# An opening stage in place of three, four modulation rows moved into projection 1, the experts' down products in split form, and their weights loaded as 8 KB by partition

## What is computed

```python
sh1, sc1, gt1, sh2, sc2, gt2 = split(silu(c) @ w_mod + b_mod, 6)       # w_mod 1024 x 6144; c_ctx likewise
h  = rms_norm(x, g_pre_mix) * (1 + sc1) + sh1                          # ctx likewise, with its own two
u, uc = h @ w_in, hc @ w_in                                            # w_in 1024 x 4544
# first experts: 16, each on its 128 best tokens
hid = silu(xs @ w_gate) * (xs @ w_up); ye = hid @ w_down * gate        # three of 1024 x 1024
# second experts: 32 of width 512, slots of 128 tokens
gate, up = split(xs @ w_gate_up); ye = (silu(gate) * up) @ w_down      # 1024 x 1024 and 512 x 1024
```

## Time and profile before

| | |
|---|---|
| three runs | 5071.03, 5068.59, 5067.89 us, median 5068.59 |
| the profiled execution | 5070.47 us, its span 5068.4 us |
| mean granted TensorE clock | 0.909 |
| busy | PE 4206.1 us (83%), DVE 2385.4 (47%), ACT 1724.3 (34%), POOL 406.9 (8%) |
| DMA | 845.85 MB, mean 167 GB/s |

### The profile page before, as it was taken

One profiled execution on the slowest core, in us unless ns is written; L12 is line 12 of the kernel. 1 busy time (PEld: TensorE's weight loads), 2 busy tenths in 40 slices (PEclk: granted clock), 3 DMA queues, 4 the chain that ended last, 5 costly groups with the idle time before them and its releaser, 6 DMA issues. The chain is left out here.

```text
span 5068.4 us, 73757 instructions
## 1 busy us (share of the span) xinstructions
PE 4206.1 (83%) x30161; PEld 2975.7 (59%) x30161; DVE 2385.4 (47%) x3865; ACT 1724.3 (34%) x3214; POOL 406.9 (8%) x376
## 2 busy tenths in 40 slices
PE   4999966869886738999949999777779886499995
PEld 1788844448885616667538444566634655266673
DVE  2211154566664665656441464316610345466664
ACT  2211022645543304444231343216610233244442
POOL 0000012210002100000000231000000000100001
PEclk7999976979998869999969999889989998799997
DMA  6222131652223419999742332231121223699997
GB/s 246 88 93 89 62 119 48 173 162 81 78 78 117 142 68 366 367 367 367 248 183 83 119 107 78 87 113 38 38 83 50 100 58 125 237 382 381 385 382 286
DMA packets 414050, 845.85 MB, mean 167 GB/s; under 512 B 35136, under 2 KB 235872, under 8 KB 410392
## 3 DMA queue, kind: packets, MB, share of 16 engines
q1 hardware_dynamic: 393240, 782.68, 43.0%
q0 software_dynamic: 12032, 41.96, 2.6%
q10 hardware_dynamic: 8448, 16.56, 1.0%
HBM read 676.74 MB, written 164.36 MB: 166 GB/s over the span
## 5 line engine op out<-in xcount | busy, mean ns | idle before, releaser
L390 PE MATMUL psum<-proj_hi,proj_w 128*128 128x512 f32 (+2 forms) x1728 | 460.7, 355 | 15.2 <-DVE proj_w L430 13.0
L2452 ACT ACTIVATE moe_hi<-moe_raw 128x2048 fp32r<-128x2048 f32 x128 | 245.0, 1917 | 301.9 <-PE psum L2403 248.7
L2660 PE MATMUL psum<-qkv_w,hT 128*128 128x512 f32 x768 | 336.2, 597 | 12.4 <-DMA qkv_w<-in_w_in 12.4
L390 PEld LDWEIGHTS psum<-proj_hi,proj_w 128*128 128x128 f32 (+1 forms) x1728 | 303.8, 188 | 65.2 <-DVE proj_w L430 13.4
L2487 DVE TENSOR_TENSOR moe_lo<-moe_raw,moe_hi 128x2048 fp32r<-128x2048 f32 x128 | 291.5, 2288 | 87.1 <-ACT moe_hi L2452 85.1
L390 PE MATMUL psum<-proj_lo,proj_w 128*128 128x512 f32 (+2 forms) x864 | 306.1, 354 | 0.0
L4028 DVE TENSOR_TENSOR moe_lo<-moe_raw,moe_hi 128x2048 fp32r<-128x2048 f32 x128 | 287.0, 2285 | 33.4 <-ACT moe_hi L3994 33.4
L2660 PEld LDWEIGHTS psum<-qkv_w,hT 128*128 128x128 f32 x768 | 145.7, 192 | 190.3 <-issue 177.5
L3994 ACT ACTIVATE moe_hi<-moe_raw 128x2048 fp32r<-128x2048 f32 x128 | 237.1, 1905 | 11.6 <-DMA moe_raw<-in_w_gate_up 11.2
L3248 PE MATMUL psum<-branches_T,mixed_w 128*128 128x512 f32 x512 | 221.9, 596 | 13.7 <-DMA mixed_w<-in_w_attn_o 13.7
L2413 PE MATMUL psum<-moe_wd,moe_hidT 128*128 128x512 f32 x512 | 224.3, 596 | 8.4 <-DVE moe_hidT L2508 8.4
(11 more groups left out here) (612 smaller groups left out, 8697.0 us busy)
## 6 DMA issues: line engine op xcount, KB each, us to landing
moe_raw<-in_w_gate_up SPq DMA_DIRECT2D x128, 1024.0 KB, 16.4
moe_raw<-in_w_gate SPq DMA_DIRECT2D x64, 1024.0 KB, 6.9
moe_raw<-in_w_up SPq DMA_DIRECT2D x64, 1024.0 KB, 7.4
moe_wd<-in_w_down SPq DMA_DIRECT2D x64, 1024.0 KB, 9.4
moe_wd<-in_w_down SPq DMA_DIRECT2D x32, 2048.0 KB, 11.0
mod_w<-in_w_mod SPq DMA_DIRECT2D x24, 1024.0 KB, 13.9
uT<-proj_out SPq DMA_DIRECT2D x35, 640.0 KB, 2.9
chunks_pr<-prim SPq DMA_DIRECT2D x40, 512.0 KB, 4.1
```

Of the source, the lines that this page charges most:

```text
L390: ins = nc.tensor.matmul(bank[e * nch + c][0:width, 0:n], l, r, start=(k == 0 and i == 0), stop=(k == KD - 1 and i == 2))
L2452: nc.scalar.activation(hi[:, n % R], raw[:, n % R], ACT.Copy).then_inc(s["hi_ready"], 1)
L2660: last = nc.tensor.matmul(bank[2 * (n % 2) + c_][:, :], hT[:, k, i * P:(i + 1) * P], w[:, m % 2, k, c_ * BANK:(c_ + 1) * BANK], start=(k = ...
```

## The change

*Opening.* `modulation` and two `norm_T` become one stage, `opening`. It loads the first 8 pieces of `w_mod` alone (shift and gain of the first norm, for c and c_ctx), then the 10 tiles of ctx and x. The rows stay on chip: small transposes turn them into columns (`gs`). ScalarE's and VectorE's work on the tiles is the same as before.

*Later rows.* The other four rows (`Later`) are made in `gemm_T`, from 32 pieces of 128 x 1024 that are loaded into the free `hT`, ring of 4. VectorE, after each group's copy and split, does three pieces (`w * c + total`, a column of silu(c) by partition); after 8 pieces TensorE sums over partitions with a column of ones, two products of one column by 512 into banks 6 and 7, before groups 4, 7, 9 and 12, and VectorE finishes the row, SP stores it.

*Experts.* Both use one ring for all weights (`raw`, 8 and 10 pieces of 1 MB), and `w_down` pieces pass `top` and `rest` like the others. `hid` transposed is split too (`hT_hi` by ScalarE, `hT_lo` by VectorE). Down is then 48 split products in the first experts, 24 in the second. A piece's rows are laid out by `(p k) n`: partition p holds rows 2p and 2p+1, one stretch of 8 KB, and the transposes of tokens and `hid` take every other column to match. In the second experts the store of an expert's `ye` now stands in SP's order behind the loads of the third expert after it.

```diff
-def modulation(nc, bank, w_mod, b_mod, cvec, gains, mod, tables):
+def opening(nc, bank, cst, w_mod, b_mod, cvec, gains, tables, sc, ctx, x, hT):
...
-                for i in range(SETS * KD):
+                for i in range(KD):
                     if i >= R:
                         sp.wait_ge(used, i - R + 1)
+                    sp.dma_start(w[:, i % R, :], w_mod[0, i * P:(i + 1) * P, 0:PIECE]).then_inc(w_in[i % R], 16)
+                for i in range(N):
+                    src = ctx[i * P:(i + 1) * P, :] if i < NTC else x[(i - NTC) * P:(i - NTC + 1) * P, :]
+                    sp.dma_start(xt[:, i, :], src).then_inc(x_in[i], 16)
...
+                dve.wait_ge(b_in, 16 * 2 * COLT)
+                dve.wait_ge(gain_in, 16 * COLT)
+                dve.wait_ge(used, KD)
+                for j in range(COLT):
+                    nc.vector.tensor_tensor(m[at(j), :], bank[0][at(j), :], bias[at(j), :], ALU.add).then_inc(shift, 1)
...
+                for j in range(COLT):
+                    dve.wait_ge(cols_mm, j + 1)
+                    nc.vector.tensor_copy(gs[:, j // 2, 4 * (j % 2):4 * (j % 2) + 4, :].rearrange("p k r -> p (k r)"),
+                                          bank[(1, 2, 3, 0)[j]][:, 0:8]).then_inc(cols, 1)
...
+class Later:
+    ROWS = ((MOD_GT1, 1), (MOD_S2, None), (MOD_G2, 2), (MOD_GT2, 3))
+    PER, RING = 3, 4
...
+    def turn(self, v):
+
+        return (KD * v + KD - 1) // self.PER + 2
...
+                    if later is not None:
+                        for p in range(later.PER * g, later.PER * (g + 1)):
+                            load_piece(p + later.RING)
...
+                def sums(v):
+                    pe.wait_ge(piece_done, KD * (v + 1))
+                    for j in range(2):
+                        last = nc.tensor.matmul(bank[6 + j][32 * v:32 * v + 1, :], later.one,
+                                                actT[:, 4 + v % 2, j * BANK:(j + 1) * BANK], start=True, stop=True)
+                    last.then_inc(sum_mm, 1)
...
+                        ins = nc.vector.scalar_tensor_tensor(total, w_p, c, total, ALU.mult, ALU.add)
...
-    GU, R = 8, 4
+    RAW, R = 8, 4
...
-            return m[e, 2 * j * P:2 * (j + 1) * P, :].rearrange("(k p) n -> p k n", p=P)
+            return m[e, 2 * j * P:2 * (j + 1) * P, :].rearrange("(p k) n -> p k n", k=2)
...
+        def columns(k):
+
+            return ds(k // 2 * 2 * P + k % 2, P, step=2)
...
-                        down(e - 1)
+                        for j in range(4):
+                            of_down(e - 1, j)
...
-    GU, R, RD = 4, 6, 2
+    RAW, R = 10, 4
```

More of the change, by code:

```diff
@@ L161, in _ @@
[L161 to L172, removed]
@@ L360, in load, with load_piece @@
                         .then_inc(w_in[g % 2], 16)
+                def load_piece(p):
+                    if p >= later.PIECES:
+                        return
+                    if p >= later.RING:
+                        sp.wait_ge(piece_done, p - later.RING + 1)
+                    v, k = p // KD, p % KD
+                    c = later.column(v)
+                    sp.dma_start(actT[:, p % later.RING, 0:D], later.w_mod[0, k * P:(k + 1) * P, c:c + D])\
+                        .then_inc(piece_in[p % later.RING], 16)
                 load(0)
                 load(1)
+                if later is not None:
+                    sp.wait_ge(x_lo, KD)
+                    for v, (dst_row, gain) in enumerate(later.ROWS):
+                        c = later.column(v)
+                        sp.dma_start(row(6, v), later.b_mod[0:1, c:c + D]).then_inc(row_in, 16)
+                        if gain is not None:
+                            sp.dma_start(row(7, v), later.gains[0:1, gain, :]).then_inc(row_in, 16)
+                    sp.wait_ge(row_in, 16 * 7)
+                    for p in range(later.RING):
+                        load_piece(p)
                 for g in range(G):
@@ L376, in _ @@
             def _(pe):
+                def sums(v):
[4 more added lines that the diff above has]
+                    last.then_inc(sum_mm, 1)
                 for g in range(G):
+                    for v in range(0 if later is None else len(later.ROWS)):
+                        if g == later.turn(v):
+                            sums(v)
                     pe.wait_ge(lo_ready, g + 1)
@@ L442, in _ @@
                         rest(g + 2)
+                    if later is not None:
+                        for p in range(later.PER * g, later.PER * (g + 1)):
+                            piece(p)
+                        for v in range(len(later.ROWS)):
+                            if g == later.turn(v):
+                                finish(v)
 class Loop:
@@ L3887, in experts2_own, with turn, gate_up, down @@
         gate_bank, up_bank, h_bank, x_bank, y_bank = bank[0], bank[1], bank[2], bank[3:5], bank[5:7]
+        def turn(e):
+            return 6 * e - 2 if e else 0
+        def gate_up(e, j):
+            return turn(e) + j
+        def down(e, j):
+            return turn(e + 1) + (4 if e + 1 < E2 else 0) + j
+        def rows(m, e, j):
+            return m[e, 2 * j * P:2 * (j + 1) * P, :].rearrange("(p k) n -> p k n", k=2)
+        def columns(k):
+            return ds(k // 2 * 2 * P + k % 2, P, step=2)
         with nc.Block() as block:
```

556 lines of the change are left out of this document (325 added, 231 removed).

## The result

| | before | changed |
|---|---|---|
| median of 4 runs | 5069.81 us (5067.89 to 5072.50) | 4947.19 us (4941.17 to 4949.40) |
| ratio | | 0.9754, 95% interval 0.9742 to 0.9767 |
| the profiled execution | 5070.47 us | 4941.17 us, its span 4939.2 |

The forecast was 4955, its range 4915 to 5008. The time lies inside; the two expert terms do not lie where the forecast had them.

A forecast was written before the change was run, and what follows sets the result against it. In both experts stages TensorE and DMA were taken to end together; the opening filled neither. 63 - 7 + 32 + 25 = 113 us off the profiled 5070.5 gave 4957.5, adjusted to the median as 4955 us, range 4915 to 5008.

The forecast's parts named there:

- Opening, -63 forecast: Opening: projection 1 would begin at 63.9 instead of 126.8 us, saving 63 us, between 58 and 65.
- Later rows, +7 forecast: Projection 1: TensorE's sums for the four later rows add 7 us, at most 9; the rest is hidden.
- VectorE's 41 us: Projection 1: 32 VectorE operations of 1.28 us for the later rows, hidden while it waits 396 us for TensorE.
- Split down: Both experts: split down products and quicker transfers gain 32 us in the first, 25 us in the second.
- Of the period 4.2 us are lost to mixed traffic ... so I keep some 3 us: 35.3: First experts: transfers set the new period at 35.3 us, a gain of 2.0 an expert, 32 us in all.
- All three lie within 1.7 us; I take 18.4: Second experts: TensorE, VectorE and transfers nearly tie, period 18.4 us, gain 0.77 an expert, 25 us in all.
- the DMA share is 1.00 and 1.01: two resources end together: Both experts before the change: TensorE always busy and DMA full too, at about 367 and 382 GB/s.
- TensorE remains the bound: Rival for both experts, 20%: mixed stretches quicken too, gains of 45 and 45 us, time 4923 us.
- the second rival: Both experts: periods of 34.5 and 17.8 us would prove it, TensorE remaining the bound; 20%.
- the bad case: Both experts: the two-column step doubles the transposes, adding 1.6 and 1.1 us an expert, floors 36.1 and 18.9.
- The ceiling of 358 GB/s: Rival for both experts, 5%: the HBM path limits loads whatever their stretch, periods stay, time 5013 us.
- that rival's half clock: Rival for both experts, 3%: brief TensorE waits drop its clock to half, one piece each costing 131 us.

The follow-up runs named there:

- the run with dearer pieces: The changed kernel with each of the 32 later-row pieces in projection 1 passed over twice more by VectorE; 4943.57 us.
- the thinned 4 KB kernel: The changed kernel with 4 KB stretches, contiguous transposes, one split product of three in the experts and no VectorE rests of weights; 4888.34 us.
- the thinned 8 KB kernel: The changed kernel with one split product of three in the experts and no VectorE rests of weights, 8 KB stretches kept; 4887.97 us.
- small rings: The changed kernel with raw weight rings of 4 and 6 pieces instead of 8 and 10; 5042.72 us beside 5083.80 of before.
- the 4 KB run: The changed kernel with the old 4 KB weight layout and contiguous transposes, split down products kept; 4940.88 us, ratio 0.9742.

## Why the prediction was right and where it was wrong

- **Opening, -63 forecast, -64.6 found.** The eighth group of products began 1.2 us before the row that I took it from, VectorE was free at 32.5 (33.6), the ten tiles took 26.9 us (28.2), the exit 2.8 (2.1).
- **Later rows, +7 forecast.** A group of four sum instructions holds TensorE from 187.27 to 189.08 in the trace, 1.81 us, four of them 7.2. The stage is 9.1 longer, a little over the "at most 9": from its first to its last product TensorE takes 8.0 us more, and between its last product and the next stage lie 6.3 us instead of 5.2, which the sum didn't have. VectorE's 41 us were hidden as said, and the run with dearer pieces shows that the cover wasn't a near thing.
- **Split down, the work on each engine.** TensorE 34.5 and 17.8 forecast, 34.65 and 17.89 found; VectorE 32.1 and 17.3 of a period forecast, and 277.15 of 300 us are 32.0, 188.99 of 200 are 16.9. TensorE's terms were right to 0.5%.
- **The step that failed** is "Of the period 4.2 us are lost to mixed traffic ... so I keep some 3 us: 35.3" and its likeness "All three lie within 1.7 us; I take 18.4". Both rest on the first part's "the DMA share is 1.00 and 1.01: two resources end together". They did not: 4 KB transfers needed at most 34.27 of the 37.31 us. (The three of the second sentence, 17.3 to 18.7, lie within 1.4.) Of the 4.2 us, mixed traffic costs 1.2, as the thinned 4 KB kernel shows (34.27 against 33.1), and 1.1 with 8 KB (33.44 against 32.3), where I kept 3. The rest was demand: SP could issue only as slots came free, at the pace that TensorE set for VectorE (the row below, SP's waits before, 2000 to 2300 us). With either layout transfers need no more than TensorE's periods. The rival "TensorE remains the bound" (20%) had the mechanism, its 45 and 45 against 47.8 and 31.4, and its sign came true: periods of 34.5 and 17.8, which the last paragraph of the forecast ascribes to the second rival, though it stands third. Its "VectorE has 0.5 us of room in the second experts" was too generous, as the wait for `moe_hT_lo` shows.

```profile
SPq L2341 <- DVE moe_lo L2487: 200.0, 64, 6.7
```
- **Sizes within the stages.** First experts: 13 periods of 2.65 us are 34.5. The first period gave 12.1 instead of 2.65, which the forecast missed. The last period gave 2.8, the start 0.8, and the end, behind the last transposes of `hid`, took 2.4 back. Second experts: 30 periods of 1.28 are 38.5, the last gave 0.3, and the end took 6.1 back, the start 1.3. That is why the rival's 45 became 31.4 here. The forecast counted periods only.
- **The layout.** I priced it as the source of both expert gains and the step of two columns at nothing, with 1.6 and 1.1 us in the bad case. It brought nothing and cost 0.21 us an expert in the first experts; in the second 0.12 with the old down products and 0.05 beside the split. The note in the Trainium skill (SBUF: State Buffer, under Door 1) that reads within one 16-byte line go at full rate isn't borne out for TensorE's operand load, 209 ns against 139, and so the step of two floats wasn't free.
- **The ceiling of 358 GB/s** (the Trainium skill, DMA: Bandwidth & Descriptors, Where 436 GB/s comes from): the thinned 8 KB kernel moved 421 GB/s over 200 us of the second experts beside gathers and stores, the row below. Here it was no limit. The Trainium skill's page adds, under Measured, that a core gets roughly this when both cores of its pair stream; no run here has a second one.

```profile
4500.00:4700.00 200.00, 117.19 (x406) 82.82 (x407) 44.09 (x72) 154.25 (x117) 11.14 (x12) 0.80 1.02 421
```
- **The clock** stayed at 1.00 in the experts, where TensorE had no gaps. With small rings it waited 14 of 300 us and had 0.98; that rival's half clock would have needed far longer waits.
- **Why the total was close all the same** is in part luck. The experts gave 79 us instead of 57, and the named stages together 134.7 instead of 113. Of that, 5.5 us went in the middle stages and the combination, within their scatter, which leaves the 129.2 between the traces; and the changed kernel's profiled execution is the fastest of its four, 6.0 us under their median. So the medians lie 122.6 us apart, and it is 4947 instead of 4955, though the term of the experts was off by two fifths.

## What to carry to other kernels

A busy share of 1.00 on the DMA engines over a whole stage isn't a bound by itself: look at who waits for data, and for how long, in the engine that takes it first. If it waits for a consumer's buffer instead, longer stretches buy nothing, and whatever the layout costs elsewhere is a loss. How much room there is, a run with the arithmetic thinned out tells: 3.0 us an expert before, 0.2 after the split. When a separate buffer is merged into a ring, depth and the order of everything in that queue (a store behind loads too) can be worth more than the arithmetic that was changed: here 105 us between rings of 4 and 6 pieces and rings of 8 and 10, and nothing between 6 and 8 pieces and 8 and 10.

## What was not expected of the hardware

The issue of a gather on GpSimd takes 2.40 us in the second experts of the changed kernel, and 0.95 before and where VectorE's rests are left out. The changed kernel, then the thinned one (ns min/median/max):

```profile
L4106 POOL DMA_INDIRECT moe_xs<-h,slot x11: 2381/2398/2407, 4503.3 to 4682.2; - x11
```

```profile
L4103 POOL DMA_INDIRECT moe_xs<-h,slot x12: 944/947/947, 4499.8 to 4691.2; - x12
```

It has nothing to do with the layout, since the 4 KB run has 2.36 to 2.53 in the same stretch. What decides is the VectorE operation that runs when the gather's issue starts. In the changed kernel it is a subtraction of a weight's rest, which reads two SBUF tiles; then the same in the kernel with the small ring, VectorE first:

```profile
4500.37 4.49 DVE L4214 TENSOR_TENSOR moe_lo<-moe_raw,moe_hi 128x2048 fp32r<-128x2048 f32 x2
4503.30 2.38 POOL L4106 DMA_INDIRECT moe_xs<-h,slot  x1 [15.50 <-PE psum L4115]
```

```profile
4594.23 6.69 DVE L4214 TENSOR_TENSOR moe_lo<-moe_raw,moe_hi 128x2048 fp32r<-128x2048 f32 x3
4598.66 3.08 POOL L4106 DMA_INDIRECT moe_xs<-h,slot  x1 [19.03 <-PE psum L4115]
```

The issue ends 0.82 us after the subtraction in both (4505.68 and 4504.86; 4601.74 and 4600.92), and so it does for all 28 of the changed kernel's 30 gathers in this stage that start during one. Before, the operation beside it was `moe_xl`, which reads PSUM and one SBUF tile, and the issue took 0.95. With the small ring the issues of 0.94 us in the midst of subtractions are those where the running one ended 0.08 to 0.11 us after their start. In the four of 3.08 it ended 0.06 us after the start, the next had begun already, and the issue waited for that one. The Trainium skill (SBUF: State Buffer, SBUF: two separate sides) describes an exclusive lock between GpSimd and some operations of VectorE, those with two SBUF inputs among them, where the later one waits for the whole instruction of the first. The rows agree for GpSimd waiting; a subtraction that began with such an issue took 2.30 to 2.33 us instead of 2.28, so it was held for some hundredths of a microsecond and not for the 0.94. It cost nothing here, as the gather is an expert ahead; with one in the path it would be 1.5 us each time, an estimate from 2.40 less 0.95.
